# Value products in two passes, and a written order of items in six of eight stages, in a two-layer transformer kernel

## What is computed

```
x = x + 0.5 * swiglu(rmsnorm(x))                       # width 2816
o_nsa  = for each of 16 heads (4 groups of 4, head width 64):
           g0 * softmax(q kc) vc  +  g1 * softmax(q ks) vs  +  g2 * softmax(q kw) vw
o_conv = gated causal convolution of width 3
o_mem  = 4 heads of width 256 over 256 memory rows
x = x + (g_nsa*o_nsa + g_conv*o_conv + g_mem*o_mem) @ w_out
x = x + 0.5 * swiglu(rmsnorm(x))
# second layer
o_a = 16 heads of width 64, windowed softmax with a sink, 2 key heads ; o_a @ w_attn_o
o_g = gated linear attention, 4 heads, 64-row chunks                  ; o_g @ w_gla_o
x = x + (g_a*(..) + g_b*(..)) @ w_mix_o
x = x + memory attention (4 heads of width 64) ; x = x + swiglu(rmsnorm(x)) ; rmsnorm
```

## Time and profile before

| | |
|---|---|
| median of 3 runs | 2477.7 us (2474.43 to 2478.12) |
| the profiled execution | 2476.85 us, its span 2475.1 us |
| PE busy | 2420.4 us (98%) |
| PE weight loads | 2022.4 us (82%) |
| DVE busy | 1399.1 us (57%) |
| ACT busy | 982.4 us (40%) |
| POOL busy | 177.0 us (7%) |
| mean granted TensorE clock | 0.994 |

### The profile page before, as it was taken

One profiled execution on the slowest core, in us unless ns is written; L12 is line 12 of the kernel. 1 busy time (PEld: TensorE's weight loads), 2 busy tenths in 40 slices (PEclk: granted clock), 3 DMA queues, 4 the chain that ended last, 5 costly groups with the idle time before them and its releaser, 6 DMA issues.

```text
span 2475.1 us, 30790 instructions
## 1 busy us (share of the span) xinstructions
PE 2420.4 (98%) x11788; PEld 2022.4 (82%) x11788; DVE 1399.1 (57%) x2842; ACT 982.4 (40%) x1820; POOL 177.0 (7%) x244
## 2 busy tenths in 40 slices
PE   9999999999999989999999999999999998999998
PEld 7888889788887878878888888878888887888887
DVE  6435456675557676775443446667645566643444
ACT  4223235432335565663322334555422345422332
POOL 0000000100001221220000000222200002000000
PEclk9999999999999999999999999999999999999999
DMA  4454443333321111112233234211122332223222
GB/s 153 110 131 132 106 135 129 98 107 103 102 94 57 63 47 57 59 52 98 99 91 108 94 100 122 77 52 60 52 77 94 129 119 69 94 84 109 97 86 93
DMA packets 86378, 231.32 MB, mean 93 GB/s; under 512 B 8488, under 2 KB 23464, under 8 KB 86234
## 3 DMA queue, kind: packets, MB, share of 16 engines
q1 hardware_dynamic: 81072, 221.42, 27.7%
q10 hardware_dynamic: 5162, 7.95, 2.1%
HBM read 217.80 MB, written 11.53 MB: 93 GB/s over the span
## 4 chain that ended last, share of the span: by engine, by line
PE 90%; DVE 4%; ACT 3%; issue 2%; POOL 0%; DVEq 0%; ACTq 0%
PE bank L981 88%; PE bank L1197 1%; ACT t_pp L1643 1%; DVE t_pp L2170 0%; ACT t_tmp L1490 0%; PE bank L1042 0%; DVE t_wlo L1915 0%; ACT t_PS L1490 0%; ACT t_whi L1490 0%; DVE t_PS L1920 0%; PE bank L1371 0%; DVE t_ST L2443 0%; ACT t_pw L1643 0%; DVE t_KS L2299 0%; DVE t_tmp L2278 0%
## 5 line engine op out<-in xcount | busy, mean ns | idle before, releaser
L981 PE MATMUL bank<-t_XH,t_whi 128*128 128x512 f32 x2064 | 814.0, 394 | 9.2 <-DVE t_sa L2170 2.8
L981 PE MATMUL bank<-t_XH,t_wlo 128*128 128x512 f32 x2064 | 805.0, 390 | 0.0
L981 PE MATMUL bank<-t_XL,t_whi 128*128 128x512 f32 x2064 | 804.6, 390 | 0.0
L1915 DVE TENSOR_TENSOR t_wlo<-t_raw,t_whi 128x1024 fp32r<-128x1024 f32 (+2 forms) x418 | 478.7, 1148 | 359.0 <-ACT t_whi L1490 356.0
L1490 ACT ACTIVATE t_whi<-t_raw 128x1024 fp32r<-128x1024 f32 (+3 forms) x422 | 415.9, 988 | 420.6 <-PE bank L981 366.9
L981 PEld LDWEIGHTS bank<-t_XH,t_whi 128*128 128x128 f32 x2064 | 388.4, 188 | 92.3 <-DVE t_sa L2170 4.2
L981 PEld LDWEIGHTS bank<-t_XH,t_wlo 128*128 128x128 f32 x2064 | 388.2, 188 | 82.0
L981 PEld LDWEIGHTS bank<-t_XL,t_whi 128*128 128x128 f32 x2064 | 388.8, 188 | 78.0
L981 PE MATMUL bank<-t_RX,t_whi 128*128 128x512 f32 x1056 | 325.1, 389 | 0.0
L2032 DVE TENSOR_TENSOR t_tmp<-bank,t_RB 128x512 f32<-128x512 f32 x178 | 122.5, 688 | 219.2 <-PE bank L981 214.2
L981 PEld LDWEIGHTS bank<-t_RX,t_whi 128*128 128x128 f32 x1056 | 198.2, 188 | 41.3
(11 more groups left out here) (324 smaller groups left out, 2726.1 us busy)
## 6 DMA issues: line engine op xcount, KB each, us to landing
t_raw<-in_f_in SPq DMA_DIRECT2D x86, 512.0 KB, 3.3
t_raw<-in_f_out SPq DMA_DIRECT2D x32, 384.0 KB, 3.1
t_raw<-in_w_conv SPq DMA_DIRECT2D x24, 512.0 KB, 3.3
t_raw<-in_w_merge SPq DMA_DIRECT2D x24, 512.0 KB, 3.3
t_raw<-in_fg SPq DMA_DIRECT2D x22, 512.0 KB, 3.3
t_raw<-in_fu SPq DMA_DIRECT2D x22, 512.0 KB, 3.3
t_raw<-in_f_out SPq DMA_DIRECT2D x32, 320.0 KB, 3.0
t_raw<-in_w_g SPq DMA_DIRECT2D x16, 512.0 KB, 3.3
```

The costliest lines, as they stand in the source:

```text
L981: return e.matmul(o, l, r, start=start, stop=stop, skip_group_check=True)
L1915: e.tensor_tensor(wlo[n % NRAW][:, 0:width], raw[n % NRAW][:, 0:width], f32(whi[n % NHI][:, 0:width]), ALU.subtract).then_inc(*w_lo.tick(n))
```

## The change

1. **Two passes for values.** `VS`, `VC` and the window heads' tile hold, for a head's 64 value columns, the rounded part and the rest side by side as one stationary operand of 128 columns. `two` streams the rounded and the rest part of the probabilities over it. The upper 64 rows of the bank then hold (rounded values)·p and the lower 64 (rest of values)·p. Each head has a bank of its own. ACT copies the lower half out (`slow`, `oalow`), DVE adds the two halves (`both_halves`) into a tile `OC`/`OC2`, from which the merge, or the rounding and the rest of `oa`, now read. The compressed branch of a pair is two `two` over 512 columns. The zero fill shrinks to `VC`.
2. **Written order.** `timed` rearranges the items of stages 0, 1, 3, 4, 5 and 6 by the word lists in `TIMES`. Items of one name keep their order among themselves.
3. `smerge`, `oalow`, `oasum` and `oa` go through `w.later`; `attend` counts 6 and 4 in place of 8 and 6 for a head's values.

Compared with the order before, the lists of stages 0 and 5 are the same, word for word. In stages 1, 3, 4 and 6 they differ, but the sequence of the dense units and so of the weight loads is the same in all of them; what moves are the small items between them. Stage 1 has 8 new items (`slow`), stage 3 has 32 (`oalow`, `oasum`).

```
+TIMES = {
+    6: """
+        mv2 nspread mq2x mq2s mq2x mq2 score score mv2 mq2s mv2s weigh score weigh score scale weigh weigh score score
+        score scale weigh score scale scale turn weigh scale score weigh rest scale turn score weigh scale rest turn
...
+def timed(items):
+    out, part, stage = [], [], -1
+    def close():
+        if stage in TIMES:
+            waiting = {}
+            for item in part:
+                waiting.setdefault(item[0][0], []).append(item)
+            named = TIMES[stage].split()
+            assert len(named) == len(part)
+            part[:] = [waiting[kind].pop(0) for kind in named]
...
-                    own += {"spa": 8, "mem": 12, "win": 6, "mm2": 6}[hd.kind]
+                    own += {"spa": 6, "mem": 12, "win": 4, "mm2": 6}[hd.kind]
...
-                            w.add("smerge", 2 * g + p, w.first_merge(2 * g + p), n)
+                            w.later.append(one("slow", 2 * g + p, n))
+                            w.later.append(lambda: w.add("smerge", 2 * g + p, w.first_merge(2 * g + p), n))
...
+                    w.later += [one("oalow", n), one("oasum", n)]
+                    if r % 2:
+                        w.later.append(one("oa", 2 * g + r // 2))
...
-    VS = place("VS", 5120, 5120, F32R).rearrange("p (a c j n) -> p a c j n", a=2, c=2, j=4)
+    VS = place("VS", 5120, 2048, F32R).rearrange("p (a j g n) -> p a j g n", a=2, j=4, g=2)
+    OC, OT = place("OC", 7168, 512), [place(f"OT{q}", 7680 + 512 * q, 512)[0:64, :] for q in range(2)]
...
+        def two(o, l, rh, rl, start, stop):
+            mm(o, l, rh, start, False)
+            return mm(o, l, rl, False, stop)
...
-                o = take("ov", ("out", n)) if first else banks[("out", n - q)]
+                o = take("ov", ("out", n)) if a == 0 else banks[("out", n - 1)]
...
-                    f = three(o[:, j * P:S], VS[:, a, 0, j, c:c + P], VS[:, a, 1, j, c:c + P],
-                              ph[:, j * S:(j + 1) * S - j * P], pl[:, j * S:(j + 1) * S - j * P], first and j == 0, False)
-                if final:
+                    f = two(o[:, j * P:S], VS[:, a, j, g % 2, :], ph[:, j * S:(j + 1) * S - j * P],
+                            pl[:, j * S:(j + 1) * S - j * P], a == 0 and j == 0, False)
+                if q == 3:
...
-                    f = three(o, VC[0][:, p, :], VC[1][:, p, :], PCT[0], PCT[1], False, True)
+                    for x in range(2):
+                        f = two(banks[("out", n - 3 + 2 * x)], VC[:, r - 1 + x, :], PCT[0], PCT[1], False, True)
...
+        def slow(m, n):
+            on.wait_ge(*full.at(("values", n)))
+            for x in range(2):
+                on.wait_ge(*evac.at(("os", n - 7 + 2 * x)))
+                copy(OT[x], banks[("out", n - 3 + 2 * x)][64:128, :]).then_inc(*copied.tick(("ot", n - 3 + 2 * x)))
...
         def smerge(m, first, n):
-            on.wait_ge(*full.at(("values", n)))
-            merge(m, 0, first, T[4], ("sgate", m), banks[("out", n - 3)], ("free", ("out", n - 3)))
+            on.wait_ge(*evac.at(("taken", m - 1)))
+            for x in range(2):
+                both_halves(OC[64 * x:64 * x + 64, :], n - 3 + 2 * x, OT[x])
+            on.wait_ge(*evac.at(("os", n - 1)))
+            merge(m, 0, first, T[4], ("sgate", m), OC, ("taken", m))
...
+        def both_halves(o, n, x):
+            on.wait_ge(*copied.at(("ot", n)))
+            e.tensor_tensor(o, banks[("out", n)][0:64, :], x, ALU.add).then_inc(*evac.tick(("os", n), ("free", ("out", n))))
...
-            low(OAL[:, m, :], banks[("out", WIN0 + 2 * m)], OAH[:, m, :], ("oa", 0, m), ("free", ("out", WIN0 + 2 * m)))
+            low(OAL[:, m, :], OC2, OAH[:, m, :], ("oa", 0, m))
...
-            e.memset(f32(VS), 0.0)
-            e.memset(f32(VC[0]), 0.0)
-            e.memset(f32(VC[1]), 0.0).then_inc(*cleared.tick("sparse"))
+            e.memset(f32(VC), 0.0).then_inc(*cleared.tick("sparse"))
```

## The result

| | before | after |
|---|---|---|
| median of four runs | 2476.06 us (2474.22 to 2478.12) | 2400.21 us (2398.12 to 2401.5) |
| ratio | 1 | 0.9687 [0.9675, 0.9699] |
| span of the profiled execution | 2475.1 us | 2398.5 us |
| PE idle in the span | 54.7 us | 24.9 us |

The change makes the kernel 3.1% faster, 75.9 us.

A forecast was written before the change was run, and what follows sets the result against it. The prediction took the kernel as bound by PE's own work plus some 45 us in which the in-order chains of DVE, ACT and POOL keep PE waiting. Its sum was 2476.85 - 26.7 (work) - 20 (order) = 2430 us, range 2406 to 2456.

The forecast's parts named there:

- Two passes on PE: Sparse and window values: fewer matmuls save 20.8 and 7.7 us, compressed branch adds 1.8; PE's work falls by 26.7 us.
- All of this is on the path: Sparse and window parts: the whole 26.7 us less PE work shortens the kernel, since PE is the bound there.
- Copies and additions: Sparse and window heads: 22.0 us added on DVE and 20.2 on ACT, of which 2 us exposed on PE's path.
- The handover rival (2492): Banks 6 and 7 and window banks: copies plus additions come onto PE's path, 42.2 us, giving 2492 us; chance 0.04.
- The written order: Attention stretches: reordered items remove 20 us of PE's 45.1 us of stops, net of 2 us for exposed additions.
- The second rival: Attention stretches: the order takes nearly all stops, 42 us, with sparse clock at 1.00, giving 2408 us; chance 0.15.

The follow-up runs named there:

- e9: Changed kernel in its written order, with one matmul repeated for each key tile of the sparse and window heads: 2424.47 us, ratio 0.9788 to the kernel before.
- e1: Changed kernel without its written tables, items in the planner's order with the new ones put through `w.later`: 2494.17 us, ratio 1.0073 to the kernel before.
- e10: Two-pass values in the item list of the kernel before, copies, additions and merges directly behind their values pass: 2495.74 us, ratio 1.0078 to the kernel before.
- e2: Kernel before, with three-pass values, in the written order and without the new items: 2420.14 us, ratio 0.9779 to the kernel before.
- e16: e10 with rest parts left out, copies and additions on an idle SBUF tile, copies waiting for the values pass, additions for the copies: 2490.72 us, ratio 1.0062.
- e13: e10 with rest parts left out, as many copies and additions run on an idle SBUF tile, waiting for nothing from PE: 2473.49 us, ratio 0.999.

## Why the prediction was wrong, and where it was right

**Two passes on PE: right.** The passes take 1.30 and 0.97 us, the counts are 256, 128 and 32, and the repeated pass adds 28.5 us to PE's busy time and 24.3 to the kernel's, where 28.5 were worked out. The spacing in the Trainium skill ("TensorE: Matmul & The Clock Gate", section "Back-to-back issue gap") would have given 0.54 us less for a sparse pass; the trace has 1.95 - 1.30 = 0.65, so the rows of before were the better source.

**"All of this is on the path": right only in the written list.** There the passes bring 19.9 us; copies and additions take some 2.5, and the remaining 4.3 us to 26.7 went into stops (PE idle for 21.2 us in e9, 24.9 in after). In the old list they bring nothing and cost 20 us. The prediction summed passes and order as if each kept its value without the other.

**Copies and additions: 2 us taken, some 2.5 measured,** again in the written list alone and not clear of noise, so the agreement says little. The durations were right to 1% on DVE and 10% on ACT. The reason given was not: DVE's free 30% is no cover for an in-order engine. In the old list DVE is free for as much time and the same operations cost 30.6 us, 8.3 as load, 18 through the wait of the addition for the copy. The prediction named the place, `weigh` and `rest` queued behind the additions, but gave it no price: the link stood in its sum only as a chain of the handover, with its bound on the distance between passes (10.6 us), which is a bound for the bank and not for DVE. The distance between the items takes this wait away, and it is free only where it does not make a release late, as it does in e1.

**The handover rival (2492): wrong here; its wait exists without the tables, at a fifth of its price.** After has no such wait; e1 has it three times, 7.9 us. That e1 lands at 2494.2, beside the rival's 2492, is luck: the rival put 42.2 us on this wait, and most of e1's 81.1 us of idle time lies elsewhere. The mechanism in e10 is its neighbour, DVE behind the copy. The prediction's five to nine small items between a pair's last `values` and its `smerge` are a misreading: the written list has 1 to 17 items there, 11 in the median.

**The written order: the step that failed.** The term was -20 us, "less than half of what there is", where there were 45.1 us. It measured -55.9 (the additions' 2 us aside), more than all there was: 44.9 us in stage 1 (743.0 to 698.1) and 9.5 up to the first matmul on `OA`, where the prediction had 13 for the sparse part and 6 for the memory and window parts together. Two errors lie in it. The bound was too narrow: it counted the stops by PE's idle time and left out what goes with the stops, the time at half clock (9.9 us less lost in e2) and the drain (some 7), though the granted clock of 0.98 and 0.93 in the earlier trace rows stood in the evidence. And the choice within it was too low. I counted margins between `score` and `turn`, found them shrinking in most tiles of the sparse part, and took this as half a veto. The count gave no warning of the outcome: the stops went all the same. What the traces do show is that DVE stands less before ACT in the sparse part: before, then e2, in DVE's waits (total, times, longest):

```profile
DVE t_wlo L1915 <- ACT t_whi L1490: 28.1, 25, 4.4
DVE t_PS L1920 <- ACT t_PS L1490: 17.9, 30, 1.8
```

```profile
DVE t_wlo L2057 <- ACT t_whi L1632: 18.6, 20, 3.3
DVE t_PS L2062 <- ACT t_PS L1632: 12.0, 23, 1.4
```

That is 15 us less of standing for the same links. It may be a result as much as a cause, since the stretch is itself over 30 us shorter. Which of the moved items brings the gain was not tried one by one, and stays open. In e2 PE's stops in the sparse stretch, 742 to 1068 us, are 326.00 - 322.11 = 3.9 us, against 27.2 in before:

```profile
742.00:1068.00 326.00, 322.11 (x1876) 281.75 (x1875) 250.72 (x759) 210.20 (x543) 88.74 (x136) 1.00 0.19 65
```

The second rival, with 0.15, named this case, the clock at 1.00 included, but had priced it at 42 us of idle time alone, so even its 2408 was too high.

**No wait became the new bound.** PE is busy for 99% of the span. In the second memory attention 3.9 us of stops are left (forecast 3.9).

## What to carry to other kernels

The price of a small operation on an in-order engine is more than its duration (8.3 us for all 64 in the old list): how long the engine stands before it counts too (18 us). So when a step needs a copy on one engine and then an addition on another, put other items between the two, and read the idle time in front of the group. Then look for who waits for the result: the same items can make a release late, and in e1, where DVE hardly stood, the operations still cost 21.5 us. What PE loses in these traces is its idle time, plus half of the time in which it works at the lower clock, plus a drained matmul at each stop; a bound by idle time alone is too low. And don't add the gains of less work and of a better order: here the first was worth -20 us or +20 us, by the second.

## What was new about the hardware

A stop of 2.5 us is followed by 3.4 us at a granted clock of 0.50, in a kernel whose PE is 98% busy; I had not reckoned with that. Of the six stretches of before, four have a stop of 1.7 to 2.5 us or several of 0.65 to 1.4 close ahead, one (638.6) begins just after a stop of 1.8, and one (775.1) has a stop of 0.88 behind 16 matmuls of two columns. After has one with no stop ahead of it at all, at 401.6 us; its timeline, then the two windows around the fall:

```profile
397.81 2.73 PE L1132 MATMUL bank<-t_cst,t_tmp 128*128 128x1 f32 x24
400.40 0.48 PE L1132 MATMUL bank<-t_MX,t_whi 128*128 128x256 f32 x2
```

```profile
398.00:401.50 3.50, 3.50 (x32) 3.50 (x32) 2.54 (x11) 1.70 (x3) 0.00 (x0) 1.00 0.51 153
401.70:405.00 3.30, 3.30 (x18) 3.30 (x17) 2.92 (x15) 0.07 (x1) 0.00 (x0) 0.50 0.00 0
```

The row says 100% busy on both sides; what the engine did before the fall was 24 matmuls of a single column each. So not every stretch is a stop's doing, and how many of them the stops alone make was not measured. All twelve stretches of e10 have a stop of 0.9 us or more close ahead or around their start; the one at 916.9 us begins within a stop of 2.96 us. The longer stretches in the records are 6.8 us. e10 and e16 have 54.6 and 64.9 us of them before 2300 us. PE works for 48.0 and 59.8 us of these, so 24.0 and 29.9 us of time are lost while PE is recorded as busy. With this the old list's numbers nearly close: from before to e10 the profiled span grows by 16.1 us, and -26.7 (work), +28.4 (idle time), +12.6 (half of 25.2 us more of work at half clock) and +2.5 (15 more gaps of 0.17 us) make +16.8. Reading one operand of 64x512 from PSUM costs DVE nothing here (680 and 679 ns in after, 745 and 679 in e13 with both operands in SBUF), and ACT copies the shape faster out of a bank, 595 and 589 ns, than out of SBUF in e13, 618 and 616.
